# A transformer pair in fp32: DSA logits by two heads and all rows in one block, the table of positions in two fp32r parts, and the output projection with the DSA blocks second

## What is computed

```python
# DSA: keys that the indexer selects; 8 heads of 64; bias by distance of positions
bucket = t5_bucket(jnp.maximum(t[None, :, None] - idx, 0))
bias = rel_bias[bucket]
logits = einsum('bthd,btkhd->bthk', qb, k_sel) * (dh ** -0.5) + bias
probs = softmax(logits); ha = einsum('bthk,btkhd->bthd', probs, v_sel)
# end of the first block
ha = ha.reshape(B, S, A_WIDTH) * silu(a_z)
h = h + concatenate([hm, ha], -1) @ w_out        # hm: 1024 wide, ha: 512 wide
# second block, for each layer i
mod = (silu(c) @ mod_w[i] + mod_b[i]).reshape(B, 6, D)
hin = x * (1 + mod[:, 1]) + mod[:, 0];  y = mixer(hin)
x = layer_norm(ALPHA * x + mod[:, 2] * y)
hin = x * (1 + mod[:, 4]) + mod[:, 3];  y = conv_ffn(hin)
x = layer_norm(ALPHA * x + mod[:, 5] * y)
```

## Time and profile before

| | |
|---|---|
| median of 3 runs | 892.44 us (892.40 to 892.50) |
| the profiled execution's own time | 892.48 us |
| its span in the trace | 890.6 us |
| TensorE busy | 857.5 us, 96% |
| VectorE busy | 668.7 us, 75% |
| ScalarE busy | 452.5 us, 51% |
| GpSimd busy | 68.0 us, 8% |
| DMA | 201.00 MB, mean 226 GB/s |

### The profile page before, as it was taken

One profiled execution on the slowest core, in us unless ns is written; L12 is line 12 of the kernel. 1 busy time (PEld: TensorE's weight loads), 2 busy tenths in 40 slices (PEclk: granted clock), 3 DMA queues, 4 the chain that ended last, 5 costly groups with the idle time before them and its releaser, 6 DMA issues.

```text
span 890.6 us, 14511 instructions
## 1 busy us (share of the span) xinstructions
PE 857.5 (96%) x5768; PEld 754.0 (85%) x5768; DVE 668.7 (75%) x1090; ACT 452.5 (51%) x720; POOL 68.0 (8%) x62
## 2 busy tenths in 40 slices
PE   8999989999999999999999999899999999999996
PEld 8988978767876898699999999579987899999995
DVE  5598798878976997789757857796777876556557
ACT  5564554454546545275544545265563664444450
POOL 1000001000001120011200100110000111001011
PEclk9999999999999999999999999999999999999999
DMA  9756666555965780799866896389717886646601
GB/s 342 291 165 192 206 234 219 189 165 196 346 222 233 251 293 1 316 332 380 286 228 216 284 351 238 99 268 332 230 47 287 295 300 198 205 164 190 190 1 48
DMA packets 57028, 201.00 MB, mean 226 GB/s; under 512 B 6600, under 2 KB 7936, under 8 KB 56960
## 3 DMA queue, kind: packets, MB, share of 16 engines
q1 hardware_dynamic: 55952, 196.89, 63.2%
q0 software_dynamic: 1008, 3.18, 1.2%
HBM read 198.96 MB, written 1.08 MB: 225 GB/s over the span
## 4 chain that ended last, share of the span: by engine, by line
PE 81%; DVE 11%; ACT 4%; issue 2%; POOL 1%; DMA 0%; DVEq 0%
PE ps L1165 26%; PE ps L1166 25%; PE ps L1167 25%; DVE R L1476 2%; DVE wsp L1413 1%; PE ps L1178 1%; ACT pb L2116 1%; DVE wk L1451 1%; PE ps L1342 1%; PE ps L1381 1%; PE ps L1257 1%; DVE small L1854 0%; PE ps L1350 0%; PE ps L1357 0%; DVE X L1849 0%
## 5 line engine op out<-in xcount | busy, mean ns | idle before, releaser
L1165 PE MATMUL ps<-XT,wsp 128*128 128x256 f32 x768 | 217.1, 283 | 4.3 <-DVE XT L1458 3.0
L1166 PE MATMUL ps<-XT,wsp 128*128 128x256 f32 x768 | 214.5, 279 | 0.0
L1167 PE MATMUL ps<-XT,wsp 128*128 128x256 f32 x768 | 214.2, 279 | 0.0
L1413 DVE TENSOR_TENSOR wsp<-ring,wsp 128x1024 fp32r<-128x1024 f32 x144 | 178.7, 1249 | 9.3 <-ACT wsp L1958 9.3
L1958 ACT CAST wsp<-ring 128x1024 fp32r<-128x1024 f32 x143 | 148.6, 1045 | 61.9 <-PE ps L1167 54.7
L1165 PEld LDWEIGHTS ps<-XT,wsp 128*128 128x128 f32 x768 | 144.0, 187 | 8.5 <-issue 3.9
L1166 PEld LDWEIGHTS ps<-XT,wsp 128*128 128x128 f32 x768 | 144.0, 188 | 1.0
L1167 PEld LDWEIGHTS ps<-XT,wsp 128*128 128x128 f32 x768 | 143.7, 187 | 0.0
L1165 PE MATMUL ps<-wsp,ra 128*128 128x512 f32 x236 | 94.3, 400 | 4.0 <-issue 1.5
L1167 PE MATMUL ps<-wsp,ra 128*128 128x512 f32 x236 | 93.5, 396 | 0.0
L1166 PE MATMUL ps<-wsp,ra 128*128 128x512 f32 x236 | 93.3, 395 | 0.0
(11 more groups left out here) (272 smaller groups left out, 1517.7 us busy)
## 6 DMA issues: line engine op xcount, KB each, us to landing
arena<-in_mod_w SPq DMA_DIRECT2D x50, 512.0 KB, 6.2
ring<-in_mod_w SPq DMA_DIRECT2D x42, 512.0 KB, 4.9
ring<-in_ffn_a SPq DMA_DIRECT2D x28, 512.0 KB, 5.0
ring<-in_ffn_b SPq DMA_DIRECT2D x28, 512.0 KB, 5.1
arena<-in_ffn_o SPq DMA_DIRECT2D x22, 512.0 KB, 4.7
ring<-in_ffn_o SPq DMA_DIRECT2D x22, 512.0 KB, 4.8
arena<-in_ffn_a SPq DMA_DIRECT2D x16, 512.0 KB, 5.3
arena<-in_ffn_b SPq DMA_DIRECT2D x16, 512.0 KB, 4.9
```

Source lines behind the costliest of these rows:

```text
L1165: pe.matmul(o, l[0], r[0], start=start, stop=False)
L1166: pe.matmul(o, l[0], r[1], start=False, stop=False)
L1167: return pe.matmul(o, l[1], r[0], start=False, stop=stop)
L1413: ve.tensor_tensor(w[:, 1024:1024 + n], raw[slot[0]][:, 0:n], w[:, 0:n].bitcast(f32), SUB).then_inc(*done("V", "lo", u, also=[("raw", *slo ...
```

## The change

- The table is split into an fp32r high part and a low part on VectorE, both go to DRAM (`gscr` has 16 rows) and come back as three transfers: the high part to the place of `TB`, the low part into columns 2048 to 3071 and 5120 to 6143 of `ra`, where the last third of the projection's operand is written later. ScalarE makes an fp32r copy of `anti`.
- `sc2` becomes `sc4`, at each i divisible by 4. For two heads it first issues four fp32r matmuls of 512 columns (two banks, high and low part, the 256 columns of the table read twice), then the query-key matmuls for t=0 (columns 384 to 511 of the bank) and for t=1 (columns 0 to 255). The two banks are held until both row blocks are read.
- The 12 blocks of the output projection are now `hm0`, DSA, `hm1` (the rows of `w_out` are packed accordingly). The transposes of `hm1`, the return of the pace of `modulation` to 0.8, that of `W.lag`, and the step `pt2` stand ahead of the fourth unit; before, the first three stood ahead of the third and `pt2` ahead of the fifth.

```diff
@@ dsa_steps
             if i < n:
-                if i % 2 == 0:
-                    bs = {i + e: bank.get() for e in range(2)}
-                    add("sc2", i, [bs[i], bs[i + 1]], [prior("bank", bs[i + e]) for e in range(2)])
+                if i % 4 == 0:
+                    bs = [bank.get() for _ in range(2)]
+                    add("sc4", i, bs, [prior("bank", b) for b in bs])
                 ps[i] = pb.get()
-                add("sc", "dsa", i, bs[i], None, ps[i], prior("pb", ps[i]))
-                bank.put(bs[i][0])
+                add("sc", "dsa", i, bs[i % 2], None, ps[i], prior("pb", ps[i]))
+                if i % 4 > 1:
+                    bank.put(bs[i % 2][0])
@@ before_out
         if q == 2:
+            W.finish(dsa)
+        if q == 3:
             transposed("hm1", 4, None)
             mod[0][1], W.lag = MOD_PACE[0], LAG
-            W.finish(dsa)
-        if q == 4:
             add("pt2")
@@ buffers
-        gscr = nc.dram_tensor("gscr", [8, 384], f32, kind="Internal").ap()
+        gscr = nc.dram_tensor("gscr", [16, 384], f32, kind="Internal").ap()
-        TB = grid(ra[:, 6144:8192], 8)
+        TB = [[c + h * 256 for c, n in at for h in range(n)]
+              for at in (((6144, 8),), ((2048, 4), (5120, 4)))]
@@ tensor
-                elif kind == "sc2":
+                elif kind == "sc4":
                     i, bs, before = a
                     for e_, b in enumerate(bs):
-                        n, [(l, r, events)] = head("dsa", i + e_)
-                        for e in new("P", events, before):
+                        for e in new("P", ("tb", 0), ("tb", 1), ("tb", 2), ("anti",), before):
                             pe.wait_ge(*e)
-                        pe.matmul(ps[b[0]][:, 0:n], l, r, start=True, stop=False)
-                    for e_, b in enumerate(bs):
-                        for e in new("P", ("tb",), ("misc",)):
-                            pe.wait_ge(*e)
-                        pe.matmul(ps[b[0]][:, 0:n], anti, TB[:, of("dsa", i + e_)[0], 256 - n:256].bitcast(f32),
-                                  start=False, stop=True).then_inc(*done("P", "fill", *b))
+                        for q in range(2):
+                            c = TB[q][of("dsa", i + e_)[0]]
+                            pe.matmul(ps[b[0]], antir, bass.AP(ra, c, [[8192, 128], [0, 2], [1, 256]]), start=q == 0,
+                                      stop=False)
+                    for t in range(2):
+                        for e_, b in enumerate(bs):
+                            n, [(l, r, events)] = head("dsa", i + 2 * t + e_)
+                            for e in new("P", events):
+                                pe.wait_ge(*e)
+                            ins = pe.matmul(ps[b[0]][:, 384 * (1 - t):384 * (1 - t) + n], l, r, start=False, stop=t == 1)
+                            if t:
+                                ins.then_inc(*done("P", "fill", *b))
@@ vector
-                    ve.tensor_copy(grow, ps[b[0]][0:8, 0:384]).then_inc(*done("V", "grow", also=[("bank", *b)]))
+                    ve.tensor_copy(grow[0].bitcast(f32r), ps[b[0]][0:8, 0:384]).then_inc(*done("V", "grow", 0))
+                    for e in new("V", ("grow", 0)):
+                        ve.wait_ge(*e)
+                    ve.tensor_tensor(grow[1].bitcast(f32r), ps[b[0]][0:8, 0:384], grow[0], SUB).then_inc(
+                        *done("V", "grow", 1, also=[("bank", *b)]))
@@ scalar
+                elif kind == "tb":
+                    for e in new("A", ("misc",)):
+                        ac.wait_ge(*e)
+                    ac.copy(antir, anti).then_inc(*done("A", "anti"))
```

More of the change, by code:

```diff
@@ L982, in build @@
         msum = [t[:, :] for t in msum_t]
-        small = sb("small", 512)
+        small = sb("small", 288)
+        antir = sb("antir", 128, f32r)[:, :]
         arena = sb("arena", 14866)
@@ L1083, in ready @@
             if x == "mx":
-                return ("xt", "hm0", k) if k < 4 else ("xt", "hm1", k - 4) if k < 8 else ("fin_dsa", k - 8)
+                return ("xt", "hm0", k) if k < 4 else ("fin_dsa", k - 4) if k < 8 else ("xt", "hm1", k - 8)
             if x in ("ot0", "ot1"):
@@ L1090, in split_of @@
         def split_of(tag):
-            return {"cq": (CT, 0), "hm0": (MX, 0), "hm1": (MX, 4)}.get(tag, (XT, 0))
+            return {"cq": (CT, 0), "hm0": (MX, 0), "hm1": (MX, 8)}.get(tag, (XT, 0))
         def source(tag, t, k):
@@ L2128, in scalar @@
                         ac.wait_ge(*e)
-                    ac.copy(MX[0][8 + k], wk[s[0]][:, 0:256]).then_inc(*done("A", "fin_hi", k))
+                    ac.copy(MX[0][4 + k], wk[s[0]][:, 0:256]).then_inc(*done("A", "fin_hi", k))
                 elif kind == "fin_o":
@@ L2272, in pool @@
                 elif kind == "grow":
-                    for e in new("G", ("grow",)):
-                        po.wait_ge(*e)
-                    po.dma_start(gscr, grow).then_inc(*done("G", "tg", by=16))
-                elif kind == "tb":
-                    for e in new("G", ("tg",)):
-                        po.wait_ge(*e)
-                    po.dma_start(TB.bitcast(f32), bass.AP(gscr.tensor, 0, [[1, 128], [384, 8], [1, 256]])
-                                 ).then_inc(*done("G", "tb", by=16))
+                    for q in range(2):
+                        for e in new("G", ("grow", q)):
+                            po.wait_ge(*e)
+                        po.dma_start(gscr[8 * q:8 * q + 8], grow[q]).then_inc(
+                            *done("G", "tg", q, also=[("tg",)] if q else [], by=16))
+                elif kind == "tb":
+                    for e in new("G", ("tg", 0), ("tg", 1)):
+                        po.wait_ge(*e)
+                    for q, (c, h, n) in enumerate(((6144, 0, 8), (2048, 8, 4), (5120, 12, 4))):
+                        po.dma_start(grid(ra[:, c:c + n * 256], n), bass.AP(gscr.tensor, h * 384, [[1, 128], [384, n], [1, 256]])
+                                     ).then_inc(*done("G", "tb", q, by=16))
                 elif kind == "one":
```

18 lines of the change are left out of this document (10 added, 8 removed).

## The result

The changed kernel takes 895.57 us (median of 5 runs, 895.03 to 897.74) where the kernel before takes 892.50 in the same session: ratio 1.0034, 95% interval 1.0021 to 1.0047. It is about 3 us slower, by more than the 0.2% that can be told apart. The forecast was 898.1 with a range of 893.2 to 901. The profiled execution is the slowest of the five: 897.74 us, span 895.9.

The account below looks back on a forecast made before the run. TensorE was taken to bound the kernel, busy 857.5 of 890.6 us. The terms -1.4 + 1.9 - 0.5 + 5.4 + 0.2 = +5.6 us on 892.5 gave 898.1 us, range 893.2 to 901.

Parts of the forecast that it names:

- Part 1: DSA bias matmuls: the split table in fewer blocks saves TensorE time, less a stall; -1.4 us, bounds -2.4 to -0.5.
- four groups at 0.45, -1.8: DSA: each of four two-head groups gains 0.45 us from cheaper table matmuls and fewer fp32 entries; -1.8 us, bounds -1.6 to -2.4.
- 0.16 a group: DSA: allowance of about 0.16 us for two entries in a group's old blocks, within the gain taken as 0.45.
- the stall: DSA: TensorE waits on VectorE's backlog for norm 9 and transpose 11, so the gain is -1.4 us, not -1.8.
- by the end of the m_z pair TensorE is 0.34 us later: DSA, after the third block: TensorE is 0.34 us later there, where VectorE starts a backlog that TensorE and ScalarE release.
- Part 2: Output projection: the new block order makes TensorE wait for low parts and puts VectorE behind; +1.9 us, bounds +0.7 to +2.3.
- The +0.7 of TensorE's own: Output projection: TensorE is 3.05 us off pure work against 2.37 now, with stalls of 1.5 and 0.6 us; +0.7.
- The other +1.2: End of the output projection: VectorE's closing additions to X come 1.8 to 2.2 us later, and x1's transposes wait on them.
- Part 3, vector (0,3): Modulation, before x1: vector (0,3) moves one unit on, removing a TensorE wait of 0.49 us; -0.5 us.
- Part 3, the load chain: `mla_o` to first FFN: `mod_one`(0,4) two units later delays SyncE's loads, `ffn_a` and the residual; +5.4 us, bounds +4 to +6.
- attention, +0.2 forecast: Attention: vector (0,4)'s VectorE steps shift among the attention steps; -0.5 to +1 us, taken +0.2.
- Rival D: Gap before the first FFN block: the clock falls as well, 1 to 2.5 us on top of +5.6, 899 to 901; chance 0.12.

Follow-up runs that it names:

- e1: The changed kernel run once more, unaltered: 895.18 us, ratio 1.0018 to the kernel before.
- after: The changed kernel in its first measurement and profile, against the kernel before: 895.57 us, ratio 1.0034.
- e4: The changed kernel's split table alone; the output projection keeps the order and pace of the kernel before: 887.03 us, ratio 0.9912.
- e9: The split table alone, as in e4, with `small` at 384 columns so later tiles lie where the kernel before has them: 890.70 us, ratio 0.9976.
- e2: The changed kernel with the modulation's pace set back ahead of the third output projection unit, as in the kernel before: 887.89 us, ratio 0.9923.
- e11: The changed kernel with the second modulation pace 0.70 instead of 0.65, returning `mod_one`(0,4) to its old place: 890.43 us, ratio 0.9977.
- e3: The kernel before with the modulation's pace set back one output projection unit later, ahead of the fourth: 902.18 us, ratio 1.0083.
- e5: The kernel before with only the memory layout of the changed kernel, `arena`, `ra` and later tiles 384 bytes per partition lower: 888.78 us, ratio 0.9956.
- e10: The kernel before with `small` at 384 columns, so `arena`, `ra` and later tiles lie 512 bytes per partition lower: 892.70 us, ratio 1.0000.

## Why the prediction was right, and where it was not

The direction and the range held, and the main cause was named with its place: the pace returns one unit later, `mod_one`(0,4) comes two units of `mla_o` later, the loads behind it on SyncE are late, ScalarE waits for `ffn_a`, and TensorE waits for the residual. The size was closer than its parts deserve. Term by term, stages of e1 or after against the kernel before:

**Part 1, -1.4 forecast, -2.6 measured** (e4 and e9, w_moz..x1). The bound of -2.4 was passed. All but 0.1 of it lies between the entry into `w_moz` and the matmul behind the hm0 wait: 47.14 us before, 44.63 in e1 and e4. Each kind of row there, summed from start to start with the waits in brackets taken out (one profile each):

```
us                                before   e1
table matmuls                     5.51     4.36
query-key matmuls                 4.23     3.43
transposes of the probabilities   2.71     1.70
120 matmuls of the projection     29.43    28.98
values, hm0 transposes            3.36     3.53
waits                             1.90     2.63
sum                               47.14    44.63
```

The step "four groups at 0.45, -1.8" comes near the 1.95 by which table and query-key matmuls fell, but with luck: the four table matmuls of a group take 1.11 where it had 0.93, and the query-key matmuls, which it took as unchanged (0.43 + 0.64), take 0.86. What it had too small is what an interruption costs beside itself, for which it allowed 0.16 a group: 8 interruptions of the projection became 4, and each now begins with fp32r matmuls instead of fp32. The transposes in front of a logits block (0.20 to 0.27 each before, 0.03 to 0.09 in e1) and the projection's matmuls beside one became 1.45 us cheaper. How much of that is the number and how much the order no run separates. And the stall paid less: the step "by the end of the m_z pair TensorE is 0.34 us later" has the wrong sign. VectorE's backlog starts 30.30 us behind the entry (142.17 to 172.47) where it started 30.97 behind it (140.49 to 171.46), 0.67 earlier. The waits themselves came where forecast: for norm 9 (1.41), then on L1452 (1.22).

On the passes of fp32: the Trainium skill's rule ("FP8 and Floating Point Precision", section "TensorE Precision Notes") made the table work a third cheaper, the rows say 5.51 to 4.36, a fifth. The rest of the gain is outside what that rule speaks of.

**Part 2, +1.9 forecast, +0.8 measured** (e2 against e4 in w_moz..x1). Its waits came as worked out: 1.30 and 0.51 us for 1.5 and 0.6, and in the changed kernel VectorE idle for 3.07 us for 3.1. The +0.7 of TensorE's own was right. The other +1.2, VectorE still behind at X's closing additions, did not come in e2: they start 107.0 us behind the entry into `w_moz`, 106.0 in e4, so 1.0 later and not 1.8 to 2.2, and the x1 transposes don't wait at all. With the credit back, VectorE's idle time is shorter, since a `mod_v` piece (1.28 us at 213.89) stands in it, and the 0.56 us that VectorE waits at earlier additions to X in e4 are gone:

```profile
217.04 1.29 DVE L1453 TENSOR_TENSOR ra<-ps,ra 128x512 fp32r<-128x512 f32 x2 [1.87 <-ACT ra L1999]
```

In the changed kernel the delay did come; it is in the next term.

**Part 3, vector (0,3), -0.5 forecast, +0.7 measured** (x1..m00, after, e1 and e11). The wait of 0.49 is gone as forecast. But a new one took its place, one row earlier. VectorE and TensorE of the changed kernel:

```profile
243.78 1.28 DVE L1485 SCALAR_TENSOR_TENSOR R<-ring,cactr,R 128x1024 f32<-128x1024 f32 x1
...
250.40 1.28 DVE L1754 TENSOR_TENSOR X<-X,ps 128x512 f32<-128x512 f32 x2
```

```profile
251.13 1.53 PE L1182 MATMUL ps<-cst,X 128*128 128x128 f32 x12 [0.98 <-DVE X L1754]
```

The late vector has one more `mod_v` piece, 1.28 us, in front of X's additions: four between 231 and 245 us where the kernel before has three. In e1 the additions start 108.2 us behind the entry, 2.2 later than in e4: this is the delay of 1.8 to 2.2 that I had forecast for part 2, but half of it needs the late credit, which takes a piece out of VectorE's idle time and puts it in front of the additions. I had counted what left TensorE's path and not what the same shift put into VectorE's. Taken together, part 2 and this term came out right: +1.4 forecast, +1.5 measured (e1 against e4, w_moz..m00).

**Part 3, the load chain, +5.4 forecast, +5.05 and 0.84 for the clock measured; attention, +0.2 forecast, +1.0 measured** (e1 against e11, e11 against before). The term was right within 0.4 (with the first profile of the changed kernel the 5.05 are 5.71). The rows agree with the split: in e1 `mod_one`(0,4) starts 86.7 us behind the first transpose of m00, in the kernel before 80.1, in e11 81.1; so 5.6 for the two units and 1.0 that the attention had already lost. Rival D came true beside it, as a part of 0.84 us in e1 and 1.6 in e3. The Trainium skill ("TensorE: Matmul & The Clock Gate", section "What's actually happening") has the array throttled unless activity releases it, and calls the moment of the release at a kernel's start variable from run to run. The traces agree with the first: 0.60 to 0.88 of the clock in windows behind these waits. Within the kernel they show something like the second: 1.00 or 0.63 behind one and the same wait of the hm0 transposes.

**What no term held: -2.5 us in the first FFN** (-3.0 with the late pieces' 0.5 taken out). A change of a tile's size is an edit that I had priced at nothing without saying so, and e5 shows 3.0 us for it in this stage and 4.1 in the medians; the other 1.1 is in no stage of the table (its profile enters `w_moz` 1.0 us earlier, a place that scatters by more). The Trainium skill gives no reason for it: "SBUF — State Buffer", section "SBUF: two separate sides", says that the engines' side and the transfers' side of the memory cannot contend, and that TensorE never waits on another engine's port. By that rule the pace could not be lost to loads or to another engine at a port. That the places of tiles change the pace of matmuls that read XT and wsp is measured, in e5, and e9 undoes it. Whether contention is the way, against the rule, or something else, no run shows.

**The sum.** In stages of e1: -1.85 + 0.69 + 6.04 + 0.84 - 2.51 + 0.57 = +3.8 of the profile, +2.1 to +3.1 in the medians. The forecast of +5.6 was too high chiefly because of two gains that it didn't see, part 1's interruptions (-1.2) and the places (-2.5). The attention (+0.8) and the clock (+0.8), both too small in it, went the other way, and part 2's excess (1.1) and the missing wait of the late vector (1.2) cancel. That +3 lay in the range is in part luck: the loss that the prediction is about was larger than it said (7.3 us in e2), and a gain that it didn't know of hid the difference.

## What to carry to other kernels

Where credits make the order of a list, price an edit's side effects before its work: a line moved by one unit cost 7 us here, more than the edit saved, and it is found by following the in-order load queue to the first entry that waits for a moved step. Then move the work without the pace (e2), or keep only the part that pays (e4). And give a tile that changes size a run of its own, since what lies behind it moves: 4 us of 892 hung on that.

## What the runs showed of the hardware

- Places of tiles change the pace of TensorE. 128x256 fp32r matmuls ran at 0.118 or 0.114 us start to start through most of a stage of 190 us, by a shift of 384 bytes of tiles that they don't read; a shift of 512 bytes did nothing (e5, e9, e10). In a later stage the same matmuls ran at 0.118 with either placement. The cause is open.
- The clock doesn't fall in every execution of the same list. After the same wait for the banks of the hm0 transposes (1.44 us), the granted clock was 1.00 in three profiled executions and 0.63 and 0.66 in two, at 1.6 us each. In the nine executions with the split table, where that wait is 1.22 us and one of 1.41 stands 8 us ahead of it, it never fell there.
- Small fp32 matmuls among large fp32r ones cost at each border too: the first 128x512 matmul behind a block takes 0.32 to 0.42 us start to start instead of 0.23, and four interruptions that begin with fp32r instead of eight that begin with fp32 saved 1.45 us beside the 1.95 of the matmuls themselves.
